# A two-block transformer forward pass: the first w_ada columns in three parts, and a share of the weight split on GpSimd

## What is computed

```python
c_act = silu(c)
mod = c_act @ w_ada + b_ada                      # 2048 x 12288
sh1, sc1, gt1, sh2, sc2, gt2 = split(mod, 6)
h = rms_norm(x, g_mix) * (1 + sc1) + sh1
z = h @ w_in                                     # 2048 x 11344: q, k, v of two attentions, indexer, gates
```

## Time and profile before

| what | value |
|---|---|
| median of 3 runs | 2755.99 us |
| the profiled execution's own time | 2757.48 us |
| its span in the profile | 2755.7 us |
| PE busy in the span | 2659.0 us, 96% |
| DVE busy | 1784.5 us, 65% |
| ACT busy | 1293.4 us, 47% |
| POOL busy | 259.2 us, 9% |

### The profile page before, as it was taken

The page is one execution under the profiler, slowest core; times in us unless marked ns, Lnnn a source line. Parts: engine busy times, 40 slices in busy tenths (PEclk is TensorE's granted clock), DMA queues, the critical chain, the costliest instruction groups (busy, mean ns, idle before and its releaser), DMA issues.

```text
span 2755.7 us, 33415 instructions
## 1 busy us (share of the span) xinstructions
PE 2659.0 (96%) x12195; PEld 2188.8 (79%) x12195; DVE 1784.5 (65%) x1984; ACT 1293.4 (47%) x1540; POOL 259.2 (9%) x198
## 2 busy tenths in 40 slices
PE   1999999999998999999999999999989999999999
PEld 0788888888886888888888887887878888888887
DVE  6867777778777666666666855667555555555554
ACT  1435554445435444444444554555454444444443
POOL 0000000000010000000000310131001111111110
PEclk9899999999999999999999999999999999999999
DMA  9968777667866666666665555533545555555553
GB/s 371 376 229 306 263 256 235 234 225 256 300 241 217 216 208 204 209 201 198 205 206 183 175 167 185 190 123 123 199 146 190 191 190 191 190 185 195 185 196 138
DMA packets 273307, 585.39 MB, mean 212 GB/s; under 512 B 14576, under 2 KB 17036, under 8 KB 272324
## 3 DMA queue, kind: packets, MB, share of 16 engines
q1 hardware_dynamic: 273220, 584.23, 62.2%
HBM read 582.01 MB, written 2.11 MB: 212 GB/s over the span
## 4 chain that ended last, share of the span: by engine, by line
PE 91%; DMA 3%; DVE 3%; ACT 1%; issue 1%; SPq 0%; DVEq 0%; ACTq 0%
PE lin L443 28%; PE lin L445 28%; PE lin L444 28%; DMA sb_ada<-in_w_ada_dram 2%; DMA sb_raw<-in_w_in_dram 1%; DVE sb_wlo L1448 1%; DVE sb_acc L1567 1%; PE aux L738 1%; PE aux L892 1%; PE aux L473 1%; ACT sb_whi L939 1%; DMA sb_raw<-in_w_out_dram 0%; PE aux L749 0%; PE aux L522 0%; DVE sb_ada_first L1465 0%
## 5 line engine op out<-in xcount | busy, mean ns | idle before, releaser
L1448 DVE TENSOR_TENSOR sb_wlo<-sb_raw,sb_whi 128x1024 fp32r<-128x1024 f32 x896 | 1105.5, 1238 | 831.2 <-ACT sb_whi L939 828.6
L939 ACT ACTIVATE sb_whi<-sb_raw 128x1024 fp32r<-128x1024 f32 x896 | 946.7, 1060 | 1276.0 <-PE lin L445 1171.0
L443 PE MATMUL lin<-sb_whi,sb_act_hi 128*128 128x512 f32 x2720 | 1081.2, 398 | 6.9 <-DVE sb_wlo L1448 4.0
L445 PE MATMUL lin<-sb_whi,sb_act_lo 128*128 128x512 f32 x2720 | 1061.9, 390 | 0.0
L444 PE MATMUL lin<-sb_wlo,sb_act_hi 128*128 128x512 f32 x2720 | 1060.9, 390 | 0.0
L443 PEld LDWEIGHTS lin<-sb_whi,sb_act_hi 128*128 128x128 f32 x2720 | 512.1, 188 | 118.4 <-issue 11.1
L445 PEld LDWEIGHTS lin<-sb_whi,sb_act_lo 128*128 128x128 f32 x2720 | 511.7, 188 | 108.9
L444 PEld LDWEIGHTS lin<-sb_wlo,sb_act_hi 128*128 128x128 f32 x2720 | 512.4, 188 | 104.6 <-issue 2.7
L443 PE MATMUL lin<-sb_whi,sb_hid_hi 128*128 128x512 f32 x704 | 275.4, 391 | 0.0
L445 PE MATMUL lin<-sb_whi,sb_hid_lo 128*128 128x512 f32 x704 | 274.2, 389 | 0.0
L444 PE MATMUL lin<-sb_wlo,sb_hid_hi 128*128 128x512 f32 x704 | 273.9, 389 | 0.0
(11 more groups left out here) (329 smaller groups left out, 1645.6 us busy)
## 6 DMA issues: line engine op xcount, KB each, us to landing
sb_raw<-in_w_in_dram SPq DMA_DIRECT2D x88, 1024.0 KB, 6.7
sb_raw<-in_ffn_w_gu_dram SPq DMA_DIRECT2D x88, 1024.0 KB, 5.0
sb_ada_in<-in_w_ada_dram SPq DMA_DIRECT2D x128, 512.0 KB, 4.1
sb_raw<-in_gla_w_in_dram SPq DMA_DIRECT2D x48, 1024.0 KB, 5.1
sb_raw<-in_w_gate_dram SPq DMA_DIRECT2D x44, 1024.0 KB, 5.1
sb_raw<-in_w_up_dram SPq DMA_DIRECT2D x44, 1024.0 KB, 5.1
sb_raw<-in_w_down_dram SPq DMA_DIRECT2D x44, 1024.0 KB, 5.7
sb_raw<-in_ffn_w_down_dram SPq DMA_DIRECT2D x44, 1024.0 KB, 5.0
```

The costliest lines, as they stand in the source:

```text
L443: pe.matmul(o, h, whi[:, w], start=first and q == 0, stop=False)
L445: m = pe.matmul(o, l, whi[:, w], start=False, stop=last and q == 1)
L939: act.activation(whi[:, idx % RING * HALF:(idx % RING + 1) * HALF], raw[:, idx // 2 % RING, idx % 2 * HALF:(idx % 2 + 1) * HALF], ACT.Copy ...
L1448: dve.tensor_tensor(wlo[:, c], raw[:, idx // 2 % RING, idx % 2 * HALF:(idx % 2 + 1) * HALF], whi[:, c].bitcast(fp32), ALU.subtract).then_i ...
```

## The change

`EARLY` goes from 3 to 2: two quarters (kc 0 and 1) of sh1 and sc1 come first, as 16 pieces of 128x2048, then quarter 2 as 16 late pieces of 128x1024, then quarter 3 as 16 more, so 32 late pieces. Slabs 4 to 7 are each followed by 4 late pieces in place of 2, slab 8 by 8. PE makes the columns of quarter 2 before half 11 and those of quarter 3 before half 18, there with three `keep_running` between the last adds and two behind. `first_columns` multiplies with 64 columns of ones in place of 1, and the modulation reads every 64th column. The fillers at the start may begin one row block earlier. ACT makes the features of quarter 2 after its split of half 12, those of quarter 3 after half 18, directly (`first_high`). GpSimd makes the low part of halves 5, 7, 9, 11, 13, 15 and 17 with a subtraction over 128x1024; DVE keeps the even halves from 4 to 18, each but the first behind a wait for the half before, and has the adds between them in groups of 2 to 4.

```diff
@@ -27,7 +27,7 @@
...
 RING = 4
-EARLY = 3
+EARLY = 2
 SLOTS = 4
@@ -55,6 +55,7 @@
...
+WIDE = NB // 8
 EARLY_ROWS = KT - 1 + EARLY
@@ -93,7 +94,7 @@
...
     acc0 = at("acc0", [P, 2, EARLY * NB], ADA)
-    acc1 = at("acc1", [P, 2, NB], ADA + 12 * KB)
+    acc1 = at("acc1", [P, 4 - EARLY, 2, NB], ADA + 8 * KB)
     xaff = at("xaff", [P, 2, 2, S], XB)
@@ -294,12 +295,13 @@
...
-        def late_piece(kt):
-            slot, place = kt // 2 % SLOTS, kt % 2 * 2 * NB
+        def late_piece(p):
+            slot, place = p // 2 % SLOTS, p % 2 * 2 * NB
+            c0 = (EARLY + p // KT) * NB
             last = KT - SLOTS + slot + 1 if slot < SLOTS - 1 else EARLY_ROWS
-            sp.wait_ge(sem("ada0_sum"), last if kt < 2 * SLOTS else EARLY_ROWS + kt // 2 * 2 - 2 * SLOTS + 2)
-            sp.dma_start(ada0[:, slot, place:place + 2 * NB].rearrange("p (b n) -> p b n", b=2), w_first[kt * P:(kt + 1) * P, :, EARLY * NB:D]
+            sp.wait_ge(sem("ada0_sum"), last if p < 2 * SLOTS else EARLY_ROWS + p // 2 * 2 - 2 * SLOTS + 2)
+            sp.dma_start(ada0[:, slot, place:place + 2 * NB].rearrange("p (b n) -> p b n", b=2), w_first[p % KT * P:(p % KT + 1) * P, :, c0:c0 + NB]
                          ).then_inc(sem(f"ada0_in{slot}"), 16)
@@ -314,13 +316,14 @@
...
             first_slab(s)
-        for kt in range(2 * SLOTS):
-            late_piece(kt)
-        for s in range(RING, 12):
+        late = iter(range(2 * KT))
+        for s, pieces in ((None, 8), (4, 4), (5, 4), (6, 4), (7, 4), (8, 8)):
+            if s is not None:
+                first_slab(s)
+            for _ in range(pieces):
+                late_piece(next(late))
+        for s in range(9, 12):
             first_slab(s)
-            if s < RING + 4:
-                late_piece(2 * SLOTS + 2 * (s - RING))
-                late_piece(2 * SLOTS + 2 * (s - RING) + 1)
         sp.dma_start(ixw_raw[:].rearrange("p (k n) -> p k n", k=KT), w_in[:, :, C_IX:C_IX + NIXW]).then_inc(sem("ixw_in"), 16)
@@ -514,40 +517,44 @@
...
-            acc, c0 = (acc0, kc * NB) if kc < EARLY else (acc1, 0)
+            acc, c0 = (acc0, kc * NB) if kc < EARLY else (acc1[:, kc - EARLY], 0)
             if kc >= 2:
...
                 c = c0 + j % 4 * P
-                m = pe.matmul(aux[kc % 2][:, j:j + 1], acc[:, j // 4, c:c + P], ones[:, 0:1], start=True, stop=True)
+                m = pe.matmul(aux[kc % 2][:, j * WIDE:(j + 1) * WIDE], acc[:, j // 4, c:c + P], ones[:, 0:WIDE], start=True, stop=True)
             m.then_inc(sem("ada0_T"), 1)
...
-        def keep_running(count):
+        def keep_running(count, bank=3):
...
             for _ in range(count):
-                pe.matmul(aux[3][:], ident, con[:, 0:NB], start=True, stop=True)
-        pe.wait_ge(sem("ada0_sum"), KT - 3)
+                pe.matmul(aux[bank][:], ident, con[:, 0:NB], start=True, stop=True)
+        pe.wait_ge(sem("ada0_sum"), KT - 4)
         keep_running(5)
...
         keep_running(1)
-        for kc in range(2):
+        for kc in range(EARLY):
             pe.wait_ge(sem("ada0_sum"), KT + kc)
...
             for g in range(3):
-                if (kc, g) == (EARLY - 1, 2):
-                    pe.wait_ge(sem("ada0_sum"), EARLY_ROWS + KT)
-                    first_columns(EARLY)
                 for i in range(2):
+                    if (kc, g, i) == (1, 2, 1):
+                        pe.wait_ge(sem("ada0_sum"), EARLY_ROWS + KT)
+                        first_columns(2)
+                    if (kc, g, i) == (3, 0, 0):
+                        for r in (4, 3, 2):
+                            pe.wait_ge(sem("ada0_sum"), EARLY_ROWS + 2 * KT - r)
+                            keep_running(1, 0)
+                        pe.wait_ge(sem("ada0_sum"), EARLY_ROWS + 2 * KT)
+                        first_columns(3)
+                        keep_running(2, 0)
                     if g == 0:
...
                          banks=aux[2:4] if g == 2 else None)
-                    if (kc, g, i) == (0, 0, 0):
-                        pe.wait_ge(sem("ada0_sum"), EARLY_ROWS)
-                        first_columns(EARLY - 1)
@@ -1046,16 +1053,16 @@
...
                 first_high(1)
-        for kc in range(1, EARLY):
+        act.wait_ge(sem("gs_made"), 2)
+        first_pair(2)
+        first_pair(3)
+        for kc, idx0 in ((2, RING), (3, 13)):
+            for idx in range(idx0, (13, 19)[kc - 2]):
+                split(0, "A", 48, idx)
             act.wait_ge(sem("gs_made"), kc + 1)
-            first_pair(2 * kc)
-            first_pair(2 * kc + 1)
-        for idx in range(RING, 19):
-            split(0, "A", 48, idx)
-        act.wait_ge(sem("gs_made"), EARLY + 1)
-        first_high(6)
-        first_high(7)
-        pairs[0], affine[0] = KT // 2, 4
+            first_high(2 * kc)
+            first_high(2 * kc + 1)
+        pairs[0], affine[0] = KT // 2, 2
@@ -1577,15 +1584,15 @@
...
-        def late_add(kt):
-            slot, place = kt // 2 % SLOTS, kt % 2 * 2 * NB
-            dve.wait_ge(sem(f"ada0_in{slot}"), 16 * (KT // SLOTS) + 32 * (kt // (2 * SLOTS)) + 32)
-            acc, new = acc1[:].rearrange("p b n -> p (b n)"), ada0[:, slot, place:place + 2 * NB]
+        def late_add(p):
+            slot, place, kt = p // 2 % SLOTS, p % 2 * 2 * NB, p % KT
+            dve.wait_ge(sem(f"ada0_in{slot}"), 16 * (KT // SLOTS) + 32 * (p // (2 * SLOTS)) + 32)
+            acc, new = acc1[:, p // KT, :, :].rearrange("p b n -> p (b n)"), ada0[:, slot, place:place + 2 * NB]
             if kt == 0:
...
             else:
-                dve.wait_ge(sem("ada0_sum"), EARLY_ROWS + kt)
+                dve.wait_ge(sem("ada0_sum"), EARLY_ROWS + p)
                 m = dve.scalar_tensor_tensor(acc, new, cact[:, kt:kt + 1], acc, ALU.mult, ALU.add)
@@ -1593,8 +1600,10 @@
...
             dve.wait_ge(sem("ada0_T"), kc + 1)
-            dve.tensor_tensor(sh_mix[:, c], aux[kc % 2][:, 0:4], b_sh1[:, c], ALU.add)
-            link(dve.tensor_tensor(gs_mix[:, c], aux[kc % 2][:, 4:8], b_sc1[:, c], ALU.add))
+            columns = aux[kc % 2][:].rearrange("p (j w) -> p j w", w=WIDE)
+            column = lambda v: v.rearrange("p (k a) -> p k a", a=1)
+            dve.tensor_tensor(column(sh_mix[:, c]), columns[:, 0:4, 0:1], column(b_sh1[:, c]), ALU.add)
+            link(dve.tensor_tensor(column(gs_mix[:, c]), columns[:, 4:8, 0:1], column(b_sc1[:, c]), ALU.add))
             dve.scalar_tensor_tensor(gs_mix[:, c], gs_mix[:, c], 1.0, g_mix[:, c], ALU.add, ALU.mult).then_inc(sem("gs_made"), 1)
@@ -1627,23 +1636,41 @@
...
         split(0, "A", 48, 2)
-        first_modulation(2)
         split(0, "A", 48, 3)
-        late_add(0)
-        late_add(1)
-        for idx in range(RING, 18):
+        def late_features(kc):
+            first_modulation(kc)
+            dve.wait_ge(sem("gs_made"), kc + 1)
+            for g in (2 * kc, 2 * kc + 1):
+                first_affine(g)
+                first_low(g, xaff[:, g % 2, :, :])
+        def even_split(idx, adds):
+            if idx > RING:
+                dve.wait_ge(lo_made, idx)
             split(0, "A", 48, idx)
-            late_add(idx - 2)
-            if idx in (5, 6, 11, 12):
-                g = {5: 2, 6: 3, 11: 4, 12: 5}[idx]
-                first_low(g, xT[:, 2 * g:2 * g + 2, :])
-        split(0, "A", 48, 18)
-        first_modulation(3)
-        dve.wait_ge(sem("gs_made"), 4)
-        for g in (6, 7):
-            first_affine(g)
-            first_low(g, xaff[:, g % 2, :, :])
-        pairs[0], affine[0] = KT // 2, 4
+            for p in adds:
+                late_add(p)
+        even_split(4, range(0, 2))
+        for g in (2, 3):
+            first_low(g, xT[:, 2 * g:2 * g + 2, :])
+        for p in range(2, 6):
+            late_add(p)
+        even_split(6, range(6, 8))
+        even_split(8, range(8, 12))
+        even_split(10, range(12, 16))
+        even_split(12, ())
+        late_features(2)
+        for p in range(16, 20):
+            late_add(p)
+        even_split(14, range(20, 24))
+        even_split(16, range(24, 28))
+        even_split(18, range(28, 32))
+        late_features(3)
+        pairs[0], affine[0] = KT // 2, 2
@@ -2209,6 +2236,13 @@
...
+        for idx in range(RING + 1, 18, 2):
+            c = slice(idx % RING * HALF, (idx % RING + 1) * HALF)
+            pool.wait_ge(hi_made, idx + 1)
+            pool.wait_ge(lo_made, idx)
+            pool.tensor_tensor(wlo[:, c], raw[:, idx // 2 % RING, idx % 2 * HALF:(idx % 2 + 1) * HALF], whi[:, c].bitcast(fp32), ALU.subtract
+                               ).then_inc(lo_made, 1)
         def sb_stage(h, u):
...
```

## The result

| | before | changed |
|---|---|---|
| median of 5 runs | 2757.07 us | 2770.18 us |
| lowest and highest | 2754.12 to 2758.37 | 2769.36 to 2773.91 |
| profiled execution, its time and span | 2757.48, 2755.7 | 2773.47, 2771.4 |
| half 18 starts | 140.9 | 154.4 |

The ratio over all runs is 1.0054, 95% interval 1.0040 to 1.0067: slower, by 13.1 us between the medians. Half 18 moved by 13.5 us in the profile, half 24 by 14.4, half 48 by 12.9, and the span is 15.7 longer. So nearly all is lost ahead of half 18. What the rest of the program adds or gives back scatters: over the twelve profiles shown here against that of the kernel before, the shift of half 18 and that of the profiled execution's time differ by up to 3.8 us, in experiment 2 by 5.6.

A forecast was written before the change was run, and what follows sets the result against it. It took transfers as the bound until 76 us, then PE with DVE close behind; DVE's list ending at 137.8, columns and features to 142.0, and 3.9 for the clock put half 18 at 145.9: 2761.0 us, 80% range 2748 to 2770.

The forecast's parts named there:

- the sum without the clock, 142.0: Start of half 18 from the last add at 137.8 plus columns and features, before any allowance for a lower clock.
- Part 1, the early pieces: Start of the kernel: smaller pieces save 20.1 us of transfers; last early add starts at 56.5, half 0 at about 64.
- DVE's early adds shrink with the pieces and stay hidden: Start of the kernel: DVE's early adds get shorter with the pieces and add no time beside the transfers.
- it should do better: First columns and half 0: a better clock than before brings half 0 at about 64 in place of 65.6.
- Part 2, DVE's list: DVE's splits, adds and waits from 70 us up to the last add: 52 us, done at 122 without GpSimd's cost.
- Part 3, POOL: GpSimd's seven splits: DVE and POOL take turns, 2.25 us of DVE each, 15.8 in all; list ends at 137.8.
- Part 4, the transfers: Transfers behind the early pieces: last late piece at about 124, slab 9 at 127, no cost to half 18.
- this is covered as long as DVE ends at 138: Slab 9, needed by half 18: its place in SP's queue behind eight late pieces costs nothing if DVE ends then.
- The allowance of 3.9 us for the clock: Columns 2 and 3 at 1.2 GHz, 1.6 us more each, plus 0.7 for half 18; between 0 and 5.6.
- POOL's operation is longer: Rival, chance 0.35: GpSimd's splits decide from 2.32 us each, kernel slower; 2763 at 2.56 us, 9 us more at twice 1.77.
- POOL hides: Rival, chance 0.20: GpSimd's splits cost DVE little, half 18 at 129.5 to 135, kernel faster at 2745 to 2750.
- The clock stays up: Rival, chance 0.10: wide columns and fillers keep PE's clock up; half 18 at 142, 2757, no measurable difference.

The follow-up runs named there:

- experiment 2: Changed kernel with a GpSimd memset in place of its subtraction, low part of the seven odd halves left out; 2760.98 us, ratio 1.0013.
- experiments 4: Changed kernel with slab 9 issued ahead of the last four late pieces in place of behind them; 2769.17 us, ratio 1.0043.
- experiment 5: Changed kernel with late adds going into two running sums in turn, which PE adds up when making the columns; 2774.67 us, ratio 1.0064.
- experiment 8: Changed kernel with more fillers on PE: four ahead of columns 2, eight in place of three ahead of columns 3; 2766.92 us, ratio 1.0033.
- experiment 1: Changed kernel with the seven odd splits back on DVE, placed among the adds, nothing on GpSimd; 2763.39 us, ratio 1.0022.
- experiment 3: Kernel before, with only GpSimd making the low part of the odd halves 5 to 17; 2768.54 us, ratio 1.0032.
- experiment 7: Changed kernel with one column of ones in place of 64; 2772.27 us, ratio 1.0053.
- Experiment 9: Changed kernel without GpSimd, odd splits among the adds, slab 9 earlier, more fillers ahead of columns 2, columns 3 and the first columns; 2757.59 us, ratio 1.0004.
- kernels 6 and 10: Kernel before with 64 columns of ones in place of one, 2753.96 us; the same with two more fillers ahead of the first columns, 2754.91 us.

## Why the prediction was wrong

The place was right: what half 18 lost, the kernel lost, and the side was right too. Half 18 was forecast at 145.9 and came at 154.4, 2770 in place of 2761. The steps that failed are terms of DVE's list and of its start: the early adds put at nothing (with the clock of the first columns, 4.1 us), a late add priced at 1.19 (4.2 us), the wait for columns 2 (1.8) and slab 9 as covered (1.8). Against the sum without the clock, 142.0, there are 12.4 us to explain.

**Part 1, the early pieces: 1.8 us late, and the first columns 2.3 more.** The step that failed is "DVE's early adds shrink with the pieces and stay hidden". From 41.11 DVE has seven of them in a row, 2.44 us each, and waits for no piece; the transfers fall from 418 to 389 GB/s, which fits places that come free too late (argued, not tried). A piece of 1 MB at 418 GB/s takes 2.5 us, and DVE needs 2.44 for it: there was no margin. The last early add starts at 58.3, not 56.5. Then "it should do better", said of the clock, failed in this execution: the first columns took 3.63 us at 1.2 GHz, half 0 came at 67.9, not 64. In experiments 4, 5 and 8 it did do better, and half 0 came at 64.7 to 65.0; which of the two an execution gets was not foreseen and is not explained. DVE's list begins at 74.1, not 70.

**Part 2, DVE's list.** Two terms were too small. An add was priced at 1.19, from a row in which a split stands between two adds. Four in a row take 5.44, 1.34 each with the step to what follows, since each waits for the sum before it; experiment 5 gives it back by taking that wait away. Over the six groups of four and two shorter ones this is 4.2 us. The wait for columns 2 was 2.63, not 0.8, because of the clock: 1.8 us, and experiment 8 takes 1.7 of it away.

**Part 3, POOL.** The mechanism is confirmed (experiments 1 to 3), and its size was nearly right: 1.95, 1.92, 1.95, 1.95, 2.15, 1.93 and 1.95 over what the same DVE work takes alone, 13.8 in all, where 15.8 was forecast. Where it met no add first, POOL's operation took 2.42; where it is 3.3, the rest is its wait for DVE's first add. Doing the same on DVE would cost 7 x 1.13 = 7.9, so giving it away costs DVE 6 us more than keeping it. The rule of the Trainium skill, SBUF — State Buffer, section Who interferes with whom, fits: two inputs on DVE and reads on POOL shut each other out, and the memset, which reads nothing, left the adds at 5.45 for four. What the forecast had not named is the case of 2.15: an instruction of DVE with one tile as input was shut out as well, for 2.15 us by the subtraction and for 0.66 by the memset.

**Part 4, the transfers.** The step "this is covered as long as DVE ends at 138" failed, by 1.8 us. It priced slab 9 by its bytes, done at 127 (the 1.8 are DVE's wait for ACT's high part, 1.84). But it stands in SP's queue behind pieces that wait for adds, and so it is late by as much as DVE is: issued at 132.6, landed at 140.4. The faster DVE gets, the more it matters: 2.62 us in experiment 1, 4.79 in experiment 2.

**The sum, at the last add**: 4.1 late at the start, -2.0 for POOL, +4.2 for the adds, +1.8 for columns 2, +1.8 for slab 9, 9.9 of the 10.4 by which it came behind 137.8 (148.2); 0.5 is in no term. **The end**: columns 3 at 1.2 GHz put 3.76 between the last add and the modulation in place of 1.87, 1.9 more. The allowance of 3.9 us for the clock held columns 2 and 3 rightly, but not the first ones; and its 0.7 for half 18 was met by 0.9, seen only in the start of half 19 (158.0, 3.6 later; before 2.7), so it had no place in the sum for half 18.

**The rivals.** *POOL's operation is longer* has the right side and not its reason: it decided from 2.32 us, the one that met no add first took 2.42, which at 0.7 us per 0.1 is 1.2 us over the 2.25 assumed; but what counts is the cost to DVE, and that was 1.97 in the mean, below the 2.25. Its sign, operations beyond 2.6 us that began while DVE was idle, was not seen. *POOL hides* is out; but its bound by the transfers, half 18 at 129.5 at the earliest, was too low as well: with POOL at almost no cost to DVE (experiment 2) it came at 142.4. *The clock stays up* is out: between 55 and 160 us the changed kernel's profile has 30.7 us at the low clock, before 20.5. The rule of the Trainium skill cited there (TensorE: Matmul & The Clock Gate, section HAM oscillation: a kernel that waits for data between short bursts of products falls back each time) agrees with this trace in the main: in this stretch the clock fell five times. Not every wait did it: in experiment 2 PE was idle for 1.61 us ahead of columns 2, and they took 2.00, at full clock.

What the sum missed lay on the same side in nearly every term, since each was taken at its value without the others: an add that waits for nothing, a transfer that nothing queues ahead of, columns at full clock. The range ended at 2770 because its upper end came from one rival alone and had none of this on top.

**What stays open.** Which part of PE's work keeps the clock up is not settled. The 64 columns held it over the second set wherever the first stood at full clock (experiment 7); the same first columns stood at either level in different profiles. That the early adds hold the transfers up was not tried. Experiment 9 moved four things at once. And no version is clearly faster than the kernel before: kernels 6 and 10 are 2.2 and 1.6 us lower in the median, with intervals that reach to 1.0000.

## What to carry to other kernels

Work given to GpSimd that reads SBUF, while VectorE has a queue of instructions with two SBUF inputs, cost VectorE most of the operation, so compare that cost (here 1.95 us) with doing it oneself (1.13) and not with zero. An earlier start is worth nothing if the work that must be finished at a later point is the same: DVE had the same splits and adds ahead of half 18, so 20 us at the start became idle time of PE, which then also lost its clock. Price an operation from a row with the same neighbour ahead of it, and a transfer from the point at which its queue lets it go.

## What was unexpected of the hardware

- Adds of 128x1024 into the same sum, one behind the other, start 1.38 to 1.39 us apart; into two sums in turn 1.20, and an instruction of another kind starts 1.19 to 1.20 behind an add.
- POOL's subtraction of 128x1024 with fp32r output takes 2.42 us when DVE is just finishing, and shows as 3.3 where it begins in DVE's add; to DVE it costs 1.92 to 1.95 there, 2.15 where it ran its 2.42, and 2.2 where the instruction it shuts out is a low part of 128x512 (experiment 3).
- A POOL memset of 128x1024 takes 0.96 us and leaves DVE's adds at 5.45 for four, but a DVE TENSOR_SCALAR of 128x1024 that began just behind it took 1.41 in place of 0.75.
- A set of columns (16 passes) with 64 columns takes 1.89 to 2.00 us at 2.4 GHz and 3.67 at 1.2; with one column 1.84 to 1.96 and 3.41. The width is hidden at full clock.
- In the kernel before, 64 columns in place of one kept the granted clock at 1.00 through the stretch from 72 to 92 us, and half 18 came 4.5 us earlier. In all profiles whose first columns stood at full clock, the second ones took 3.41 with one column (three profiles) and 1.89 with 64 (seven).
